# A two-layer decoder trunk: qcT ahead of the turned queries, and the copy of turned probabilities ahead of the row maximum

## The chip, the core and the metric

The kernel runs on one core of a Trainium2 chip. The metric is the device time of one execution in microseconds. A core has five engines with a queue each: PE (TensorE, matmuls and transposes), DVE (VectorE), ACT (ScalarE), POOL (GpSimd) and SP (SyncE, which here issues the weight loads). Each queue runs in order; the program orders work between engines with semaphores written out by hand.

## The reference

Two layers of a decoder, 256 tokens of width 1024, float32. In outline, for layer 0:

```
xn   = rms_norm(h)
q, k, v, qc = split(xn @ w_in)            # 12 query heads, 3 key/value heads, 4 cross heads, 64 wide
q, k = rope(q), rope(k)
self_out  = sliding-window attention (128 keys back) with a sink logit per head
cross_out = softmax(qc . km / 8) vm       # 256 memory tokens, km, vm = rms_norm(mem) @ w_mem_kv
h += rms_norm(concat(self_out, cross_out) @ w_out)
h += rms_norm(silu(xn2 @ w_gate) * (xn2 @ w_up) @ w_down)      # 3584 wide
```

Layer 1 has stick-breaking attention in place of the first one and eight experts of the same width, of which each token uses two, in place of the dense feed-forward part.

## The kernel before

The program is one block of instructions for each engine, written by hand in the order in which the engine runs them. PSUM has eight banks; `Banks` counts how often each was filled and drained. `begin(label, bank)` makes PE wait until the bank's last content was drained, `end` marks it full, and `copy(label, ...)` on ACT or DVE waits until a label is full, moves it to SBUF and marks it empty.

**Layer-0 front end on PE.** PE transposes the normed tokens to xT, multiplies them with column blocks of w_in (labels `qa`, `qb`, `vc`; helper `rows`, line 417), and then makes the queries and keys that attention wants in transposed form. The queries with rope are written by DVE into `rope_q`, which has two buffers, and PE transposes them (line 536) into the banks 5 and 0 by turns: labels `("qT", "a", 0)`, `("qT", "a", 1)`, `("qT", "b", 0)`, `("qT", "b", 1)`; with the b ones come the keys (`("kT", tt)`, line 543). The cross queries need no rope: `turned_cols` (line 428) makes `("qcT", 0)` straight from the weights and xT, in 32 matmuls, in bank 4, between the a and the b transposes. Attention begins when all of these have been copied out (line 548).

**DVE in the front end.** A loop over n = 0 to 3 (line 1394) applies rope to qa and qb, both token tiles. For n of 2 and 3 it must not overwrite rope_q before PE has transposed what is in it:

```
if n >= 2:
    dve.wait_ge(*bk.full(("qT", "a", n - 2)))
ins = dve.tensor_tensor(rope_q[:, n % 2, 0:nq * HD], ...)      # line 1414
```

Then it writes the keys (line 1418) and, after the loop, copies both `kT` to SBUF (line 1256, `copy`).

**Attention of layer 0.** Eight units u (three key/value groups and the cross heads, each for two token tiles); a unit has nk = 1 or 2 blocks of 128 keys: 1, 2, 1, 2, 1, 2, 2, 2. All engines run the units as a pipeline, in steps s:

- PE: scores(s+1) (lines 442 and 450), weigh(s-2) (line 475, values by probabilities), turn_probs(s-1) (line 461, transposes of the probabilities to banks 4 and 5, after `norm_ok` of that unit).
- DVE: row_max(s) (lines 1309 to 1316, then `max_ok`), turned_probs(s-2) (line 1256, bank 5), normalise(s-1) (lines 1322 to 1328, then `norm_ok`).
- ACT: turned_probs(s-2) (line 966, bank 4), the exponentials of s (lines 986 to 990, after `max_ok`), mixed(s-2) (line 966).

normalise(s-1) waits until ACT has taken the exponentials of that unit; the exponentials come after its row maximum. weigh(s-2) waits for both copies of the turned probabilities.

After attention come the output projection (line 417), two norms, and the feed-forward part, in which every float32 weight is cut in two parts by ACT (`w_hi`, line 1025) and DVE (`w_lo`, line 1359) and multiplied in three matmuls (lines 556 to 558). Weights arrive by SP's queue in six slots (`raw`), each of which is loaded again once its content has been used.

Of the kernel before, what the change touches and what calls it, by code (L numbers as in the profile page):

```python
# [5 lines left out]
P = 128  # L6
# [101 lines left out]
def trunk(nc, t):  # L108

    with ExitStack() as ctx:  # L110
# [102 lines left out]
        qcT = mixT[:, 6:8, :]  # L213
# [29 lines left out]
        def probsT(u):  # L243

            return (probsT0 if u < len(UNITS0) else probsT1)[:, u % 2]

        def bank(b, lo=0, hi=512):
            return psum[:, b, lo:hi]
# [97 lines left out]
        def _(pe):  # L346
# [18 lines left out]
            def begin(label, b):  # L365

                s, n = bk.fill(label, b)
                if n > 0:
                    pe.wait_ge(s, n)

            def end(ins, label):
                ins.then_inc(bk.full_sem(label), 1)
# [39 lines left out]
            def rows(label, b, srcT, tt, w, lo, hi, at=0, first=True, last=True):  # L412

                if first:
                    begin(label, b)
                for k in range(KD):
                    ins = pe.matmul(bank(b, at, at + hi - lo), srcT[:, k, tt * P:(tt + 1) * P],  # L417
                                    w.at(k, lo, hi), start=(k == 0), stop=(k == KD - 1))
                if last:
                    end(ins, label)  # L420
                return ins

            def turned_cols(label, b, w, los):

                begin(label, b)
                for i, lo in enumerate(los):
                    for k in range(KD):
                        ins = pe.matmul(bank(b, i * S, (i + 1) * S), w.at(k, lo, lo + P), xT[:, k, :],  # L428
                                        start=(k == 0), stop=(k == KD - 1))
                end(ins, label)  # L430
                return ins
# [80 lines left out]
            w = Block()  # L512
# [3 lines left out]
            w = Block()  # L516
# [3 lines left out]
            w = Block(P)  # L520
            for tt in range(NT):
                rows(("vc", tt), 6 + tt, xT, tt, w, 0, P)
            w.done(("vc", 1))
            pe.wait_ge(consts, 1)

            for n, (tag, tt) in enumerate([("a", 0), ("a", 1), ("b", 0), ("b", 1)]):
                if n == 2:
                    w = Block(2 * P)
                    turned_cols(("qcT", 0), 4, w, (0, P))
                    w.done(("qcT", 0))  # L530
                pe.wait_ge(roped, n + 1)
                label = ("qT", tag, tt)
                begin(label, 5 if n % 2 == 0 else 0)
                b = bk.at[label][0]
                for c in range(4 if tag == "a" else 2):
                    ins = pe.transpose(bank(b, c * P, (c + 1) * P), rope_q[:, n % 2, c * P:(c + 1) * P],
                                       ident[:, :])
                end(ins, label)
                if tag == "b":
                    label = ("kT", tt)  # L540
                    begin(label, 1 + tt)
                    for g in range(NKV):
                        ins = pe.transpose(bank(1 + tt, g * P, (g + 1) * P),
                                           kdup[:, tt, g, :, :].rearrange("p u c -> p (u c)"), ident[:, :])
                    end(ins, label)
# [98 lines left out]
            w = Block()  # L644
# [80 lines left out]
            w = Block()  # L725
# [16 lines left out]
            w = Block()  # L742
# [212 lines left out]
        def _(act):  # L955
# [8 lines left out]
            def copy(label, out, src, scale=None):  # L964
                act.wait_ge(*bk.full(label))
                act.activation(out, src, ACT.Copy, scale=1.0 if scale is None else scale)\  # L966
                    .then_inc(bk.empty_sem(label), 1)
# [80 lines left out]
                           bias=halfpi[:, 0:1]).then_inc(sines, 1)  # L1048
            for tt in range(NT):
                copy(("vc", tt), v[:, tt, 64:192], bank(6 + tt, 0, 128))  # L1050
            for tag in "ab":
                if tag == "b":
                    copy(("qcT", 0), qcT, bank(4).rearrange("p (c s) -> p c s", c=2))
                for tt in range(NT):
                    label = ("qT", tag, tt)
                    n = 4 if tag == "a" else 2
                    copy(label, qT[:, 0:4, tt * P:(tt + 1) * P] if tag == "a" else
                         qT[:, 4:6, tt * P:(tt + 1) * P],
                         bank(bk.at[label][0], 0, n * P).rearrange("p (c s) -> p c s", c=n))
# [33 lines left out]
            for i, (kind, b, half) in enumerate(pieces):  # L1093
                tt = half
# [58 lines left out]
            for u, _, i, tt, *_ in UNITS1:  # L1153
                mixed(u, i, tt)
# [90 lines left out]
        def _(dve):  # L1245
            links = [0]

            def link(ins):

                links[0] += 1  # L1250
                ins.then_inc(dve_chain, 1)
                dve.wait_ge(dve_chain, links[0])

            def copy(label, out, src, scale=None):
                dve.wait_ge(*bk.full(label))
                ins = dve.tensor_copy(out, src) if scale is None else \
                    dve.tensor_scalar(out, src, scale, None, ALU.mult)
                ins.then_inc(bk.empty_sem(label), 1)
# [44 lines left out]
            def row_max(u, layer, i, tt, nk):  # L1303

                K = nk * P
                for b in range(2):
                    dve.wait_ge(*bk.full(("s", u, b)))
                src = psum[:, 2 * (u % 2):2 * (u % 2) + 2, 0:2 * K].rearrange("p b (h k) -> p b h k", h=2)
                link(dve.tensor_reduce(nmax[:, u, :].rearrange("p (h b) -> p b h", b=2), src, AX.X, ALU.max))  # L1309
                if layer == 0 and i < NKV:  # L1310
                    link(dve.scalar_tensor_tensor(out=nmax[:, u, :], in0=nmax[:, u, :], scalar=-SCALE,
                                                  in1=nsinks[:, 4 * i:4 * i + 4], op0=ALU.mult, op1=ALU.min))
                    dve.tensor_tensor(esink[:, u, :], nmax[:, u, :], sinks[:, 4 * i:4 * i + 4], ALU.add)\
                        .then_inc(max_ok, 1)
                else:
                    dve.tensor_scalar(nmax[:, u, :], nmax[:, u, :], -SCALE, None, ALU.mult).then_inc(max_ok, 1)

            def normalise(u, layer, i, nk):
                for b in range(2):
                    dve.wait_ge(*bk.empty(("s", u, b)))  # L1320
                if layer == 0 and i < NKV:
                    link(dve.tensor_tensor(psum_e[:, u, :], psum_e[:, u, :], esink[:, u, :], ALU.add))
                link(dve.reciprocal(recip[:, u, :], psum_e[:, u, :]))
                for b in range(2):
                    for s2 in range(2):
                        x = probs[:, u % 2, b, s2, 0:nk * P]
                        h = 2 * s2 + b
                        ins = dve.tensor_scalar(x, x, recip[:, u, h:h + 1], None, ALU.mult)  # L1328
                ins.then_inc(norm_ok, 1)

            def turned_probs(u, nk):
                copy(("pT", u, 1), probsT(u)[:, 1, :, 0:nk, :],
                     bank(5).rearrange("p (h k q) -> p h k q", h=2, k=2)[:, :, 0:nk, :])

            def attend(units):
                for s in range(len(units) + 2):
                    if s < len(units):
                        u, layer, i, tt, keys = (units[s][x] for x in (0, 1, 2, 3, 6))
                        row_max(u, layer, i, tt, (keys[1] - keys[0]) // P)
                    if s >= 2:  # L1340
                        u, keys = units[s - 2][0], units[s - 2][6]
                        nk = (keys[1] - keys[0]) // P
                        turned_probs(u, nk)
                    if 1 <= s <= len(units):
                        u, layer, i, keys = (units[s - 1][x] for x in (0, 1, 2, 6))
                        normalise(u, layer, i, (keys[1] - keys[0]) // P)
# [30 lines left out]
            a, n = rope_s[:, 0, :, :], rope_s[:, 1, :, :]  # L1377
# [16 lines left out]
            for n, (tag, tt) in enumerate([("a", 0), ("a", 1), ("b", 0), ("b", 1)]):  # L1394
# [3 lines left out]
                x = bank(bb, 0, nh * HD).rearrange("p (h c) -> p h c", c=HD)  # L1398
# [22 lines left out]
            for tt in range(NT):  # L1421
                copy(("kT", tt), kT[:, 0:NKV, tt * P:(tt + 1) * P],
                     bank(1 + tt, 0, NKV * P).rearrange("p (c s) -> p c s", c=NKV))
            attend(UNITS0)

            def lower_f0(tt):
# [20 lines left out]
            for i, (kind, b, half) in enumerate(pieces):  # L1447
                tt = half
# [337 lines left out]
        def _(sp):  # L1786
            for tt in range(NT):
                sp.dma_start(memb[:, tt, :], t["mem"][0, tt * P:(tt + 1) * P, :]).then_inc(mem_in[tt], 16)
            def load(n, src):
                _, c, w = src.shape  # L1790
                sp.dma_start(raw_at(n, c, w), src).then_inc(raw_full[n % RAW], 16)
# [93 lines left out]
```

## Time and profile before

| | |
|---|---|
| three runs | 1522.79, 1524.44, 1525.82 us; median 1524.44 |
| the profiled execution | 1522.79 us, span 1521.1 us |
| busy | PE 1464.3, DVE 1098.4, ACT 934.0, POOL 98.7 us |
| granted PE clock, mean | 0.988 |
| layer-0 attention on DVE | 74.85 us (first maximum) to 102.8 us |
| output projection on PE | 104.61 to 132.3 us |
| PE in attention, a unit of 256 keys | mask 0.60 and scores 1.14, weigh 1.11 us |
| PE's waits ahead of weigh for DVE's copy | 0.22, 0.93, 0.88, 0.88 us (at 84.34, 96.69, 99.83, 102.97) |
| last issue of layer-0 w_in by SP | up to 46.93 us; the 512 KB loads of it landed in 4.3 us (median) |

A row of the timeline has the start (us from the start of the span), the length in us, the engine and line, the operation, what it writes and reads with its shape, how many instructions were merged, and in brackets how long the engine was idle before and what ended that. A row of the windows has the stretch, its length, the busy time of PE, PE's weight loads, DVE, ACT and POOL with the count of instructions, PE's granted clock (1.00 is full), the share of DMA time and GB/s. The chain has start, length and what ran. Waits have the engine and what it waited for: us in total, times, the longest.

### The profile page before, as it was taken

The numbers are of one execution on the slowest core, as the hardware profiler recorded it, in microseconds if no ns is written. First come the engines' busy times: TensorE is split into PE (matmuls) and PEld (weight loads), VectorE is DVE, ScalarE is ACT, GpSimd is POOL, SyncE is SP. The second block draws the span as 40 slices with busy tenths as digits, with TensorE's granted clock in tenths as the row PEclk, the third lists the DMA queues.
The fourth block names the chain that finished last, engine by engine and source line by source line (L and its number), as shares of the span: only waits on it lengthen the run. The fifth ranks groups of instructions, "written<-read, shape, count | busy, mean of one in ns | idle before, by whom it ended". The sixth has DMA issues, their size and how long they took to land.

```text
span 1521.1 us, 18595 instructions
## 1 busy us (share of the span) xinstructions
PE 1464.3 (96%) x6705; PEld 1174.1 (77%) x6705; DVE 1098.4 (72%) x822; ACT 934.0 (61%) x790; POOL 98.7 (6%) x168
## 2 busy tenths in 40 slices
PE   6988999999999789999999999999999999999997
PEld 5555888888877478888888888888888888888885
DVE  3264554544322468989899998988899889989897
ACT  2154434343235347787777777777778778777774
POOL 3001000000000112010010002002001001000000
PEclk9999999999999979999999999999999999999999
DMA  9506555554433259999999999999999999999994
GB/s 342 176 24 221 180 198 189 182 205 139 139 111 111 97 197 389 389 357 400 375 354 400 378 366 384 387 369 377 391 366 374 389 374 368 398 377 354 387 375 162
DMA packets 177595, 446.88 MB, mean 294 GB/s; under 512 B 8784, under 2 KB 17040, under 8 KB 161424
## 3 DMA queue, kind: packets, MB, share of 16 engines
q1 hardware_dynamic: 173584, 432.60, 78.0%
q0 software_dynamic: 3968, 13.69, 2.4%
q8 instruction: 28, 0.46, 0.1%
q14 instruction: 15, 0.12, 0.0%
HBM read 438.37 MB, written 7.90 MB: 293 GB/s over the span
## 4 chain that ended last, share of the span: by engine, by line
PE 90%; DVE 4%; ACT 3%; issue 2%; DMA 1%; POOL 0%; POOLq 0%; SPq 0%; ACTq 0%; DVEq 0%
PE psum L556 24%; PE psum L558 24%; PE psum L557 24%; PE psum L417 5%; PE psum L428 4%; PE psum L875 2%; ACT w_hi L1025 2%; PE psum L782 1%; DVE w_lo L1359 1%; DMA raw<-in_l_w_mem_kv 1%; DVE reg_a L1328 0%; PE psum L383 0%; PE psum L400 0%; DVE nmax L1309 0%; PE psum L807 0%
## 5 line engine op out<-in xcount | busy, mean ns | idle before, releaser
L1359 DVE TENSOR_TENSOR w_lo<-raw,w_hi 128x2048 fp32r<-128x2048 f32 x378 | 861.5, 2290 | 192.2 <-ACT w_hi L1025 191.0
L1025 ACT ACTIVATE w_hi<-raw 128x2048 fp32r<-128x2048 f32 x378 | 724.5, 1919 | 272.8 <-PE psum L558 272.7
L556 PE MATMUL psum<-w_hi,x_hi 128*128 128x512 f32 x1120 | 444.1, 396 | 10.1 <-DVE x_lo L1354 7.6
L558 PE MATMUL psum<-w_hi,x_lo 128*128 128x512 f32 x1120 | 437.9, 391 | 0.0
L557 PE MATMUL psum<-w_lo,x_hi 128*128 128x512 f32 x1120 | 437.2, 390 | 0.0
L556 PEld LDWEIGHTS psum<-w_hi,x_hi 128*128 128x128 f32 x1120 | 211.0, 188 | 55.3 <-DVE x_lo L1354 6.3
L558 PEld LDWEIGHTS psum<-w_hi,x_lo 128*128 128x128 f32 x1120 | 210.8, 188 | 45.0
L557 PEld LDWEIGHTS psum<-w_lo,x_hi 128*128 128x128 f32 x1120 | 211.3, 189 | 42.1
L556 PE MATMUL psum<-w_hi,h_hi 128*128 128x512 f32 x560 | 218.8, 391 | 0.0
L558 PE MATMUL psum<-w_hi,h_lo 128*128 128x512 f32 x560 | 217.9, 389 | 0.0
L557 PE MATMUL psum<-w_lo,h_hi 128*128 128x512 f32 x560 | 217.9, 389 | 0.0
L558 PEld LDWEIGHTS psum<-w_hi,h_lo 128*128 128x128 f32 x560 | 105.1, 188 | 21.9
L557 PEld LDWEIGHTS psum<-w_lo,h_hi 128*128 128x128 f32 x560 | 105.2, 188 | 21.5
L556 PEld LDWEIGHTS psum<-w_hi,h_hi 128*128 128x128 f32 x560 | 105.2, 188 | 21.5
L1767 POOL TENSOR_TENSOR idle<-mhalf 128x1 f32<-128x1 f32 x7 | 15.2, 2170 | 728.2 <-DVE work L1651 728.2
L1633 DVE TENSOR_TENSOR work<-work,psum 128x512 f32<-128x512 f32 x56 | 60.7, 1084 | 0.0
L1354 DVE TENSOR_TENSOR h_lo<-psum,h_hi 128x512 fp32r<-128x512 f32 x70 | 47.8, 684 | 15.0 <-ACT h_hi L1018 15.0
L1215 ACT ACTIVATE work<-psum 128x512 f32<-128x512 f32 x56 | 33.5, 599 | 39.4 <-PE psum L558 39.3
L428 PE MATMUL psum<-reg_b,raw 128*128 128x256 f32 x256 | 56.4, 380 | 0.0
L428 PEld LDWEIGHTS psum<-reg_b,raw 128*128 128x128 f32 x256 | 48.2, 190 | 6.8 <-issue 0.3
L417 PE MATMUL psum<-raw,reg_b 128*128 128x512 f32 (+2 forms) x160 | 52.3, 487 | 1.0 <-ACT reg_b L966 1.0
L1018 ACT ACTIVATE h_hi<-psum 128x512 fp32r<-128x512 f32 x70 | 41.6, 595 | 15.9 <-PE psum L875 10.8
(245 smaller groups left out, 825.9 us busy)
## 6 DMA issues: line engine op xcount, KB each, us to landing
raw<-in_l_w_gate SPq DMA_DIRECT2D x126, 1024.0 KB, 7.5
raw<-in_l_w_up SPq DMA_DIRECT2D x126, 1024.0 KB, 7.6
raw<-in_l_w_down SPq DMA_DIRECT2D x126, 1024.0 KB, 7.2
raw<-in_l_w_in SPq DMA_DIRECT2D x14, 1024.0 KB, 6.5
raw<-in_l_w_out SPq DMA_DIRECT2D x8, 1024.0 KB, 5.1
raw<-in_l_w_mem_kv SPq DMA_DIRECT2D x4, 1024.0 KB, 6.2
ys<-w_lo SPq DMA_DIRECT2D x4, 512.0 KB, 7.1
memb<-in_mem SPq DMA_DIRECT2D x2, 512.0 KB, 3.9
```

The costliest lines, as they stand in the source:

```text
L417: ins = pe.matmul(bank(b, at, at + hi - lo), srcT[:, k, tt * P:(tt + 1) * P], w.at(k, lo, hi), start=(k == 0), stop=(k == KD - 1))
L428: ins = pe.matmul(bank(b, i * S, (i + 1) * S), w.at(k, lo, lo + P), xT[:, k, :], start=(k == 0), stop=(k == KD - 1))
L556: pe.matmul(out, x[0], w[0], start=first, stop=False, skip_group_check=True)
L557: pe.matmul(out, x[0], w[1], start=False, stop=False, skip_group_check=True)
L558: return pe.matmul(out, x[1], w[0], start=False, stop=last, skip_group_check=True)
L875: ins = pe.transpose(bank(7, c * P, (c + 1) * P), hid1[:, b % 2, c * P:(c + 1) * P], ident[:, :])
L1018: act.activation(out, src, ACT.Copy).then_inc(part_hi, 1)
L1025: act.activation(w_hi[:, m % CUT, :], raw[:, n % RAW, :], ACT.Copy).then_inc(hi_ok, 1)
L1215: act.activation(act1[:, b % 2, :], bank(bk.at["g", b][0]), ACT.Silu)\
L1354: dve.tensor_tensor(out, src, high.bitcast(F32), ALU.subtract).then_inc(bk.empty_sem(label), 1)
L1359: dve.tensor_tensor(w_lo[:, m % CUT, :], raw[:, n % RAW, :], w_hi[:, m % CUT, :].bitcast(F32), ALU.subtract).then_inc(lo_ok, 1)
L1633: dve.tensor_tensor(hid1[:, b % 2, :].rearrange("p (c q) -> p q c", c=CB), act1[:, b % 2, :].rearrange("p (q c) -> p q c", c=CB), bank(bk. ...
```

## The change

Two orders are changed; no instruction is added or taken away. On PE the matmuls of `("qcT", 0)` and the wait for their weights come right after `vc`, ahead of the transposes of all rope queries, and ACT copies qcT ahead of all qT. On DVE, in a step of layer-0 attention, the copy of the turned probabilities of unit s-2 comes ahead of the row maximum of unit s.

```
@@ PE
             w.done(("vc", 1))
+            w = Block(2 * P)
+            turned_cols(("qcT", 0), 4, w, (0, P))
+            w.done(("qcT", 0))
             pe.wait_ge(consts, 1)

             for n, (tag, tt) in enumerate([("a", 0), ("a", 1), ("b", 0), ("b", 1)]):
-                if n == 2:
-                    w = Block(2 * P)
-                    turned_cols(("qcT", 0), 4, w, (0, P))
-                    w.done(("qcT", 0))
                 pe.wait_ge(roped, n + 1)
@@ ACT
+            copy(("qcT", 0), qcT, bank(4).rearrange("p (c s) -> p c s", c=2))
             for tag in "ab":
-                if tag == "b":
-                    copy(("qcT", 0), qcT, bank(4).rearrange("p (c s) -> p c s", c=2))
                 for tt in range(NT):
@@ DVE
             def attend(units):
                 for s in range(len(units) + 2):
-                    if s < len(units):
-                        u, layer, i, tt, keys = (units[s][x] for x in (0, 1, 2, 3, 6))
-                        row_max(u, layer, i, tt, (keys[1] - keys[0]) // P)
                     if s >= 2:
                         u, keys = units[s - 2][0], units[s - 2][6]
                         nk = (keys[1] - keys[0]) // P
                         turned_probs(u, nk)
+                    if s < len(units):
+                        u, layer, i, tt, keys = (units[s][x] for x in (0, 1, 2, 3, 6))
+                        row_max(u, layer, i, tt, (keys[1] - keys[0]) // P)
                     if 1 <= s <= len(units):
```

## Rows read from the trace of the kernel before

**Rows 1.** The page: busy time by engine, and the chain by engine.
```profile
PE 1464.3 (96%) x6705; PEld 1174.1 (77%) x6705; DVE 1098.4 (72%) x822; ACT 934.0 (61%) x790; POOL 98.7 (6%) x168
...
PE 90%; DVE 4%; ACT 3%; issue 2%; DMA 1%; POOL 0%; POOLq 0%; SPq 0%; ACTq 0%; DVEq 0%
```

**Rows 2.** Windows of four stretches.
```profile
72.00:74.00 2.00, 0.47 (x5) 0.14 (x4) 1.02 (x2) 1.53 (x2) 0.00 (x0) 1.00 0.90 244
...
138.00:140.00 2.00, 2.00 (x6) 1.62 (x5) 1.73 (x2) 1.08 (x1) 0.38 (x2) 0.50 1.05 397
...
260.00:400.00 140.00, 140.00 (x654) 117.23 (x654) 64.60 (x43) 52.10 (x48) 4.63 (x10) 1.00 0.50 167
700.00:800.00 100.00, 100.00 (x457) 82.68 (x456) 89.18 (x49) 76.69 (x52) 5.77 (x5) 1.00 1.02 372
```

**Rows 3.** Waits over the whole span: SP's longest, and one of PE.
```profile
SPq L1791 <- DVE w_lo L1359: 960.7, 360, 17.9
...
PE psum L475 <- DVE reg_b L1256: 2.9, 4, 0.9
```

**Rows 4.** The chain around qcT and after the output projection.
```profile
63.28 0.87 PE psum L536 x8
64.15 6.91 PE psum L428 x32
...
138.17 0.43 PE psum L557
...
143.19 0.23 PE psum L557
```

**Rows 5.** PE in order of time: transposes, scores, weigh.
```profile
63.12 1.04 PE L536 MATMUL psum<-ident,reg_a 128*128 128x128 f32 x8
...
71.44 0.38 PE L536 MATMUL psum<-ident,reg_a 128*128 128x128 f32 x2
71.66 0.49 PE L543 MATMUL psum<-ident,mixT 128*128 128x128 f32 x3
73.69 0.38 PE L442 MATMUL psum<-band_b,ident_b 128*128 128x256 bf16 x2 [1.53 <-DVE work L1256]
...
79.33 0.66 PE L461 MATMUL psum<-ident,reg_a 128*128 128x128 f32 x4 [0.78 <-DVE reg_a L1328]
...
96.69 1.12 PE L475 MATMUL psum<-reg_b,work 128*64 128x128 f32 x16 [0.93 <-DVE reg_b L1256]
97.86 1.09 PE L461 MATMUL psum<-ident,reg_a 128*128 128x128 f32 x8
...
132.15 1.04 PE L383 MATMUL psum<-ident,xn 128*128 128x128 f32 x8
...
528.72 1.94 PE L383 MATMUL psum<-ident,xn 128*128 128x128 f32 x8 [6.33 <-DVE xn L1272]
```

**Rows 6.** DVE in order of time: ropes, copies, row maximum, scalings.
```profile
63.82 0.43 DVE L1414 TENSOR_TENSOR reg_a<-reg_a 128x256 f32<-128x256 f32 x1 [9.52 <-PE psum L536]
...
66.55 0.62 DVE L1418 TENSOR_TENSOR mixT<-reg_a 128x192 f32<-128x192 f32 x2
72.14 1.02 DVE L1256 COPY work<-psum 128x384 f32<-128x384 f32 x2 [4.97 <-PE psum L543]
...
78.40 0.87 DVE L1328 TENSOR_SCALAR reg_a<-reg_a,recip 128x128 f32<-128x128 f32 x4
79.19 0.68 DVE L1309 TENSOR_REDUCE nmax<-psum 128x4 f32<-128x512 f32 x1
...
96.66 1.14 DVE L1328 TENSOR_SCALAR reg_a<-reg_a,recip 128x256 f32<-128x256 f32 x4
98.99 0.69 DVE L1256 COPY reg_b<-psum 128x512 f32<-128x512 f32 x1 [1.19 <-PE psum L461]
```

**Rows 7.** ACT in order of time: the table load.
```profile
72.27 1.28 ACT L986 ACT_TABLE_LOAD   x1
```

**Rows 8.** Groups by line and shape, 74 to 105 us: busy us, mean ns.
```profile
L990 ACT ACTIVATE reg_a<-psum,nmax 128x256 f32<-128x256 f32 x20 | 9.2, 469 | 0.6 <-DVE nmax L1316 0.5
```

## The prediction

> **What bounds the kernel now.** I read the busy line first: PE is busy for 96% of the span, DVE for 72%, and the chain that ended last is 90% PE, most of it the three matmul lines of the two feed-forward stages [rows 1]. The windows of two such stretches show PE busy for 140.00 of 140 us and for 100.00 of 100 [rows 2]. What SP, which issues the weight loads, waits for longest is DVE's w_lo (960.7 us in 360 waits), that is, for raw slots to come free [rows 3]: the transfers run ahead of the engines there. Those stages have no slack of their own that a later start could use up. They begin when the first layer's attention and output projection are done, so any microsecond added to or taken from the layer-0 front end moves the end of the kernel by one microsecond.
>
> The change touches only that front end, from 63 to 104 us. There I read the chain, then the instructions of PE and of DVE in order of time. From 63.28 to 71.06 us the chain is PE's alone [rows 4]; at 73.69 PE has waited 1.53 us for DVE's copies of kT before the first scores [rows 5]. From 78.40 to 97.8 us it is the other way round: DVE's rows follow each other with no idle time marked [rows 6], while PE and ACT wait for it. Attention is DVE-bound from its third step, s = 2, until step 7: from the scalings of unit 0 (78.40) to those of unit 6 (96.66) six steps take 18.26 us, 3.04 each. Only in steps 8 and 9, where no row maximum is left to do, does DVE idle: 1.19 us ahead of each of the two copies of turned probabilities, the first at 98.99 [rows 6].
>
> **Part A: qcT ahead of the turned queries.** No instruction is added. PE's 32 matmuls of qcT (6.91 us in the chain [rows 4]), which lay between the a and the b transposes, now follow the last vc matmul. The wait that matters is in DVE's rope loop: for n = 2 it waits until ("qT", "a", 0) is full before it writes rope_q again. Before, this was met 0.70 us after the transposes began (63.12 to 63.82), and all the rest of the b ropes, 63.82 to 66.55 + 0.62 = 67.17, 3.35 us, lay under qcT, which lasted until 71.06 [rows 4 to 6]. After, the transposes themselves start only when qcT has ended, and nothing is left to cover the 3.35 us.
>
> Before: in the chain vc ends and the transposes take over at 63.28; scores start at 73.69; 10.41 us. After, step by step from 63.28: qcT 6.91, to 70.19. From there the a transposes until DVE starts, as from 63.28 to 63.82: 0.54, to 70.73. DVE's ropes 3.35, to 74.08. PE wakes (0.06, as between the DVE scaling that ends at 97.80 and the PE row at 97.86 [rows 5, 6]) and does the five transposes of b1 and kT1: 71.44 to 71.66 + 0.49, 0.71 us, to 74.85. DVE copies kT1: the two copies took 1.02, so one 0.51, and it starts within 0.03 us if DVE is awake and within 0.5 us if it starts as slowly as at 72.14; the kT0 copy is done just ahead of it, so I take 0.1, to 75.46. From the end of the copies (73.16) to the scores (73.69) were 0.53 us, the PE queue's row of waits. Scores start at 75.99: **+2.3 us**, between +2.2 and +2.7. What is queued behind the waiting DVE instruction is both ropes of b, both copies of kT and all of attention; behind PE's wait for the ropes, the transposes and all scores. ACT's copy of qcT costs nothing: it moves ahead of the copies of qT a, which are needed only to free bank 5, and this takes two copies of 0.6 us from about 70.3, to 71.5, while b0's ropes end at 70.73 + 1.0 = 71.73. ACT's table load of 1.28 us [rows 7] now comes at about 75, still ahead of the first maximum. The block of w_in that qcT reads was issued by 46.93 us and such a load landed in 4.3 us, so its earlier use at 63.28 is covered too; its raw slots come free 0.9 us earlier, which no one needs.
>
> **Part B: turned probabilities ahead of the row maximum.** Again nothing is added. Per step DVE did row_max(s), turned(s-2), normalise(s-1); now the copy comes first. The copy needs PE's transposes of unit s-2, which can't start before normalise(s-2), the last thing DVE did in the step before. The row maximum (0.68 us for a unit of 128 keys, more for one of 256, and two small instructions) was what DVE did while PE transposed. With the copy at the head of the queue DVE stands still for that time, and row_max(s), normalise(s-1) and then ACT's exponentials stand behind it. The trace shows this price, because steps 8 and 9 already run so: 1.19 us of marked idle, plus 0.08 because successive DVE rows otherwise overlap by that (79.19 against 78.40 + 0.87), 1.27 us for a unit with eight transposes. For one with four, PE's row is 0.66 instead of 1.09 [rows 5], so 0.84. Six units, u = 0 to 5, get the new wait, three of each size: 3 x 1.27 + 3 x 0.84 = **+6.3 us**. If four transposes save half of 1.11 instead, it is 3 x 1.27 + 3 x 0.72 = 6.0. Units 6 and 7 pay what they paid.
>
> Can the displaced work be late next? Row_max(s) ends 1.2 to 1.9 us later in the step, so ACT's exponentials of s do too, but normalise(s) is a whole step further on and they take only some 2 us (four of 0.469 [rows 8], and their small ones). PE must have done scores(s+1) and weigh(s-2) before it can transpose s-1: 1.7 and 1.1 us, against a DVE step of now 3.04 + 1.05 = 4.1 us. Neither comes to bound it. What the new order gives back: PE's weigh waited 2.9 us for DVE's copies in four places [rows 3], two of them of 0.88 us in steps 8 and 9, which stay; the other two (0.93 of it at 96.69 [rows 5]) are 1.15 us together. As DVE and not PE sets the pace there, this is worth nothing, or at most 1.15 us.
>
> **Sum.** 2.3 + 6.2 = +8.5 us. The profiled execution took 1522.79 us (span 1521.1), so 1531.3 for it; it was the fastest of the three, and on the median of 1524.44 the same sum gives **1532.9 us**. Bounds of the terms: 2.2 + 6.0 - 1.15 = +7.1 and 2.7 + 6.3 = +9.0.
>
> **The clock.** PE's granted clock is full (1.00) from 60 to 134 us, also from 72 to 74 us where PE is busy for only 0.47 of 2 us [rows 2]. It falls to 0.5 (1.2 of 2.4 GHz) only after PE stood still for 4.21 us ahead of 137.40, and there 12 matmuls in the chain took 0.43 us each instead of 0.23 [rows 4], 2.4 us. The change thins PE's work: between 71.2 and 76.0 us it will be busy for 1.4 us, and in attention it will idle about 1 us more per step. I take no fall in the sum. The Trainium skill (TensorE: Matmul & The Clock Gate, section "What's actually happening") says that the throttled state is the default and that the gate goes by how busy PE has been recently. By that rule the thinned stretch could fall to 1.2 GHz; by the rows it kept 2.4 GHz through a thin stretch. This gives the first rival.
>
> **Rivals.**
> 1. The clock falls to half in the thinned stretch. Price: 2.4 us if it hits full-length work as at 137 us; if it holds through attention, transposes go from 1.04 to 1.94 us for eight (at 132.15 and, at a granted 0.50, at 528.72 [rows 5]), and they are now on the path six times: 3 x 0.9 + 3 x 0.45 = 4.1. 1535.3 to 1537.0. Against it: the 0.47-busy stretch. 15%.
> 2. The rope wait is covered after all (part A is worth 0), because the b ropes don't truly hang on the late transpose. 1530.7. Against it: DVE's 9.5 us of idle at 63.82, released by just that transpose. 6%.
> 3. Half of part B is hidden, since PE transposes bank 5 late anyway and DVE's idle is shared with another wait. 1524.4 + 2.3 + 3.1 = 1529.8. 8%.
> 4. Not slower: attention's pace is set by PE's weigh, waiting for the copies, and not by DVE. Then the earlier copy removes the 1.15 us of waits above and its own waits cost nothing: 2.3 - 1.15 = +1.2, 1525.6. It decides if a step still takes 3.04 us. Against it: DVE's rows have no gap there and PE waits in them. 6%. Faster than that needs part A to remove PE's 1.53 us wait for kT as well: 3%.
>
> **How the numbers follow.** The forecast has 62%, with a range of its own from 1530 to 1535 (the sum's bounds and the 3 us between the runs shown). About 0.2%, 3 us, is what a measurement of this kernel can tell from no change. Slower: 62 + 15 + 6 + 8 = 91, less one for a forecast gone small, 90%. Within 0.2%: rival 4 and that one, 7%. Faster: 3%. The range reaches down to rivals 2 and 3 and up to rival 1: 1528.5 to 1537.5; outside are rival 4, the faster case and the tails.
>
> **What would show it.** Right: PE's qcT matmuls directly follow vc, at about 63; DVE idles 16 us instead of 9.5 before the first b sum, which starts at about 70.7; the first scores at about 76; DVE's copies of turned probabilities carry idle time released by PE's transposes eight times instead of twice, six of them new, 0.75 or 1.19 us each; the output projection starts at about 113 instead of 104.61; every stage after that is shifted and otherwise equal. Wrong: if the scores start before 75, part A is; if a step of attention still takes 3.04 us and not 4.1, part B is; if the projection is late by 8.5 us and the end is not, the later stages had slack, or the clock's recovery after 140 us differs.

## The result, and the profile after

The changed kernel takes 1535.83 us in the median of five runs (1532.86 to 1542.44), the kernel before 1524.44. The ratio over all its runs is 1.0087 with a 95% interval of 1.0064 to 1.0109, that is +13.3 us on 1524.4, where +8.5 was forecast. Measured again later beside other kernels it was 1536.56 us, ratio 1.0077 (1.0064 to 1.0091). So the direction was right, and the size was too small. The median of the five lies inside the range given; by the ratio the time is 1537.7, and the 34 runs listed for this kernel have a mean of 1537.7 too, just above the range.

The runs point to the clock. Each lists its mean granted PE clock, and over the 34 runs the changed kernel falls into groups, with two exceptions (1538.28 us at 0.985, and the profiled one): 1533 to 1536 us at a clock of 0.985 or 0.986, 1537 to 1538 at 0.981, 1539 to 1540 at 0.979 and 1541 to 1543 at 0.980. The kernel before is at 0.987 to 0.988 in nearly all of its own. The forecast of 1532.9 describes only the fastest executions.

The profiled execution is a slower one, 1540.10 us at a mean clock of 0.981, with a span of 1538.4 us, 17.3 us above the span of before. PE in order of time:

```profile
65.92 7.07 PE L428 MATMUL psum<-reg_b,raw 128*128 128x256 f32 x32
72.83 1.04 PE L535 MATMUL psum<-ident,reg_a 128*128 128x128 f32 x8
74.56 0.44 PE L535 MATMUL psum<-ident,reg_a 128*128 128x128 f32 x2 [0.69 <-DVE mixT L1416]
74.83 0.49 PE L542 MATMUL psum<-ident,mixT 128*128 128x128 f32 x3
76.94 0.44 PE L535 MATMUL psum<-ident,reg_a 128*128 128x128 f32 x2 [1.61 <-DVE mixT L1416]
77.21 0.49 PE L542 MATMUL psum<-ident,mixT 128*128 128x128 f32 x3
78.82 0.59 PE L442 MATMUL psum<-band_b,ident_b 128*128 128x256 bf16 x2 [1.12 <-issue]
...
111.48 1.97 PE L461 MATMUL psum<-ident,reg_a 128*128 128x128 f32 x8 [0.51 <-DVE reg_a L1326]
114.32 2.00 PE L475 MATMUL psum<-reg_b,work 128*64 128x128 f32 x16 [0.88 <-DVE reg_b L1254]
```

These answer to [rows 5]. qcT comes first, then the a transposes. PE waits 0.69, 1.61 and 1.12 us where it waited 1.53 once. The chain shows where vc ends (66.09) and when the projection begins (121.61):

```profile
66.09 6.91 PE psum L428 x32
...
78.82 0.59 PE psum L442 x2
...
111.48 1.98 PE psum L461 x8
...
121.61 3.75 PE psum L417 x7
```

From the end of vc to the first scores it is 78.82 - 66.09 = 12.73 us, where the prediction's steps give 12.71. From the first scores to the projection it is 42.79 us, where it was 73.69 to 104.61, 30.92: +11.87 us, against 6.2 forecast. DVE's rows, answering to [rows 6]:

```profile
73.54 0.42 DVE L1412 TENSOR_TENSOR reg_a<-reg_a 128x256 f32<-128x256 f32 x1 [16.43 <-PE psum L535]
...
85.62 0.87 DVE L1326 TENSOR_SCALAR reg_a<-reg_a,recip 128x128 f32<-128x128 f32 x4
87.25 0.42 DVE L1254 COPY reg_b<-psum 128x256 f32<-128x256 f32 x1 [0.75 <-PE psum L461]
...
91.32 0.69 DVE L1254 COPY reg_b<-psum 128x512 f32<-128x512 f32 x1 [1.19 <-PE psum L461]
...
110.28 1.14 DVE L1326 TENSOR_SCALAR reg_a<-reg_a,recip 128x256 f32<-128x256 f32 x4
113.48 0.69 DVE L1254 COPY reg_b<-psum 128x512 f32<-128x512 f32 x1 [2.06 <-PE psum L461]
```

DVE idles 16.43 us instead of 9.52 before the first b sum, and the new waits of attention are there, 0.75 us three times and 1.19 us three times, as worked out. What was not forecast are the idle times ahead of the last two copies, in steps 8 and 9: 2.06 us in the last row, and 2.82 at 118.25, where both had 1.19. They stand behind transposes that took 1.97 us instead of 1.09. The windows say why (the seventh number after the length is the granted clock):

```profile
66.00:74.00 8.00, 7.87 (x41) 6.75 (x40) 0.46 (x2) 1.24 (x3) 0.00 (x0) 1.00 1.05 392
74.00:78.00 4.00, 1.53 (x10) 1.05 (x10) 3.63 (x11) 1.56 (x5) 0.00 (x0) 1.00 1.05 388
78.00:84.00 6.00, 5.18 (x22) 2.51 (x22) 1.63 (x5) 2.69 (x10) 0.00 (x0) 0.52 0.44 161
84.00:108.00 24.00, 16.72 (x147) 11.66 (x146) 17.52 (x58) 14.78 (x64) 0.00 (x0) 0.98 0.00 1
108.00:122.00 14.00, 10.35 (x66) 8.44 (x66) 5.83 (x15) 4.46 (x14) 0.00 (x0) 0.53 0.00 0
122.00:124.00 2.00, 2.00 (x5) 0.77 (x5) 0.00 (x0) 0.00 (x0) 0.00 (x0) 0.84 0.04 8
124.00:150.00 26.00, 26.00 (x65) 11.60 (x64) 8.29 (x5) 5.95 (x7) 1.48 (x4) 1.00 0.23 80
```

The clock falls twice to half: at the first scores, right after the stretch from 74 to 78 us in which PE was busy for 1.53 of 4 us, and again from 108 us through the last steps of attention into the projection. From 66 us to the second fall PE never waited longer than 1.61 us. After 124 us the later stages are those of before, shifted: the last 138 us of either span have the same granted clock (0.98) and PE busy for 127.47 us here and 127.12 before, and windows of 100 to 300 us from 150 us on, shifted by 17.3 us, agree within 0.1 us of PE's busy time. The 17.3 us are then 2.8 ahead of the change, 2.3 for part A, 11.9 for attention, and 0.3 behind it (the projection begins at the low clock and takes 0.5 us longer). The 2.8 don't belong to the change. They are the start of this one execution: the first weights came 0.6 us later (13.52 us against 12.92), and the first 32 matmuls took 9.36 us where the execution of before had 7.14. Such a start isn't tied to the order: those matmuls took 7.14 us in the profile of part B alone and 9.15 in that of part A alone. In the chain:

```profile
2.10 13.52 DMA raw<-in_l_w_mem_kv
...
15.76 9.36 PE psum L400 x32
```

### The profile page after: what moved, and what is told of

Same layout as the page of the kernel before. It is cut to its first block, busy times and chain, and to the rows that moved or that the text cites. A ratio compares the mean times of both kernels' runs of the same rounds, so it can differ in the third digit from the quotient of the medians.

```text
span 1538.4 us, 18595 instructions
## 1 busy us (share of the span) xinstructions
PE 1474.6 (96%) x6705; PEld 1180.7 (77%) x6705; DVE 1098.7 (71%) x822; ACT 933.9 (61%) x790; POOL 98.2 (6%) x168
## 4 chain that ended last, share of the span: by engine, by line
PE 90%; DVE 4%; ACT 3%; issue 2%; DMA 1%; POOL 0%; POOLq 0%; SPq 0%; ACTq 0%; DVEq 0%
PE psum L555 24%; PE psum L557 23%; PE psum L556 23%; PE psum L417 5%; PE psum L428 4%; PE psum L874 2%; ACT w_hi L1024 2%; PE psum L781 1%; DVE w_lo L1357 1%; DMA raw<-in_l_w_mem_kv 1%; PE psum L461 1%; PE psum L400 1%; DVE nmax L1307 0%; DVE reg_a L1326 0%; PE psum L383 0%
## 5 line engine op out<-in xcount | busy, mean ns | idle before, releaser
L555 PE MATMUL psum<-w_hi,x_hi 128*128 128x512 f32 x1120 | 444.0, 396 | 10.1 <-DVE x_lo L1352 7.6
```

The lines of the kernel that those rows point to most:

```text
L555: pe.matmul(out, x[0], w[0], start=first, stop=False, skip_group_check=True)
```

## The experiments

Times are medians; ratios are to the kernel before, which ran beside each group of experiments on the same chip (15 to 18 runs, medians 1524.29 to 1524.57 us) and five times beside the first run of the changed kernel.

| run | us | ratio (95%) | us over before | PE clock in its runs |
|---|---|---|---|---|
| changed kernel | 1535.83 | 1.0087 (1.0064 to 1.0109) | +13.3 | 0.979 to 0.986 |
| changed kernel again | 1536.56 | 1.0077 (1.0064 to 1.0091) | +11.7 | 0.980 to 0.986 |
| A alone | 1528.60 | 1.0030 (1.0019 to 1.0040) | +4.6 | 0.984 to 0.986 |
| B alone | 1534.95 | 1.0066 (1.0053 to 1.0080) | +10.1 | 0.982 to 0.986 |
| A, own buffers | 1524.82 | 1.0007 (0.9998 to 1.0016) | +1.1 | 0.987, 0.988 |
| A, filled | 1527.56 | 1.0020 (1.0011 to 1.0028) | +3.0 | 0.987, 0.988 |
| B, filled | 1531.46 | 1.0041 (1.0029 to 1.0054) | +6.3 | 0.988 |
| both, filled | 1533.70 | 1.0063 (1.0049 to 1.0076) | +9.6 | 0.988, 0.989 |
| both, rope waits filled | 1540.57 | 1.0103 (1.0088 to 1.0119) | +15.7 | 0.980, 0.981 |
| both, attention filled | 1536.65 | 1.0087 (1.0074 to 1.0101) | +13.3 | 0.985 to 0.987 |
| qcT last | 1523.02 | 0.9993 (0.9984 to 1.0002) | -1.1 | 0.987 to 0.989 |
| qcT last, filled | 1518.76 | 0.9957 (0.9943 to 0.9971) | -6.6 | 0.992 to 0.996 |
| the same, filled more | 1516.91 | 0.9947 (0.9934 to 0.9960) | -8.1 | 0.994 to 0.998 |

**Each part alone.** Part A alone is the first two blocks of the diff, part B alone the third.

> Part A alone (qcT ahead of the turned queries; attention in the old order). Theory 1, the terms add: the first scores start 12.7 us after the last vc matmul instead of 10.4, attention itself takes its 30.9 us (first scores to output projection) unless PE's clock falls in the thin stretch before the first scores; 1526.7 on a median of 1524.4, up to 1529 if the clock falls there for some 5 us. Theory 2, part A alone costs the clock: over 1530. Rival, the rope wait is covered: 1524.

> Part B alone (copy of turned probabilities ahead of the row maximum). Theory 1: first scores unchanged, attention 6.2 us longer, 37.1 us, 1530.6, six new idle times of 0.75 and 1.19 us on DVE. Theory 2, it is the thinner attention that lets the clock fall at its end: granted clock 0.50 in part of the last 15 us before the projection and in its first matmuls, up to 4 us more, 1534 to 1535. Rival, B is hidden: 1524.

Both showed more than their waits. Of part A's profile, the chain and a window:

```profile
65.00 6.91 PE psum L428 x32
...
77.74 0.58 PE psum L442 x2
...
110.74 14.40 PE psum L417 x33
```

```profile
80.00:84.00 4.00, 4.00 (x20) 2.23 (x18) 2.00 (x5) 1.60 (x9) 0.00 (x0) 0.53 0.01 5
84.00:88.00 4.00, 2.56 (x21) 1.55 (x21) 3.76 (x18) 3.74 (x19) 0.00 (x0) 1.00 0.00 0
```

With part A alone the first scores are 12.74 us behind vc, 2.3 more than before. Attention, whose order is that of before, takes 33.00 us instead of 30.92; 2.1 us go to the clock of 0.53 in its first steps. It recovers by 84 us, and the end keeps 1.00. In part B's profile, the windows of the later steps, the projection's beginning, and PE's rows there:

```profile
72.00:88.00 16.00, 10.44 (x91) 6.78 (x91) 10.69 (x34) 9.16 (x40) 0.00 (x0) 1.00 0.38 133
88.00:102.00 14.00, 9.44 (x84) 6.59 (x84) 10.44 (x31) 8.85 (x38) 0.00 (x0) 0.98 0.01 1
102.00:118.00 16.00, 13.22 (x68) 9.31 (x66) 4.53 (x14) 4.17 (x13) 0.00 (x0) 0.50 0.00 1
```

```profile
73.49 0.38 PE L442 MATMUL psum<-band_b,ident_b 128*128 128x256 bf16 x2 [1.53 <-DVE work L1256]
...
99.58 1.09 PE L461 MATMUL psum<-ident,reg_a 128*128 128x128 f32 x8 [1.22 <-DVE reg_a L1328]
...
104.05 1.97 PE L461 MATMUL psum<-ident,reg_a 128*128 128x128 f32 x8 [0.51 <-DVE reg_a L1328]
...
114.19 16.05 PE L417 MATMUL psum<-raw,mixT 128*128 128x512 f32 x32 [0.52 <-issue]
```

Attention takes 114.19 - 73.49 = 40.70 us, 9.8 more than before: 6.4 up to the scalings of unit 6 (102.86) for the waits, and 3.4 behind them for the clock, which is at half from about 102 us on. It stays there into the projection, which takes 2.1 us longer too. So each part brings a fall of its own: A the one at the first scores, B the one at the end.

**The waits without the clock.** The direct test fills PE's waits with transposes of the identity into a bank that nobody is using. Nobody reads them.

```
def warm(n, b):
    for _ in range(n):
        pe.transpose(bank(b, 0, P), ident[:, :], ident[:, :])
...
warm((0, 0, 5, 13)[n], 6)          # ahead of wait_ge(roped, n + 1); 8 more ahead of the waits before attention
...
if s in (0, 1): warm(5, 5)         # ahead of scores
warm(6, 4)                         # ahead of wait_ge(norm_ok) in turn_probs, 3 for two of the units
warm(7, bb)                        # ahead of weigh's waits for the two cross-head units
```

> The changed kernel, with 92 transposes of the identity that nobody reads put on PE where it would wait: 26 around the rope waits, the rest in attention. If the clock is what the sum lacked: granted clock 1.00 from 60 us to the end of the projection, and the sum without a clock term holds, +8.5 us, 1533, with runs closer together than the 9.6 us between the five of the changed kernel; perhaps 0.5 to 1 us more where a filler is still running when its wait ends. Rival, something else than the clock: the runs stay between 1533 and 1542, or all are slower by the filler's 10 us, 1548.

> Part A alone with fillers around the rope waits and in the first two steps of attention. If part A is 2.3 us of waits and the rest of its 4.5 us is the clock: granted clock 1.00 from 60 to 134 us and 1524.4 + 2.3 = 1526.7. Rival: 1528.6 as without fillers.

> Part B alone with the 66 fillers in attention. If part B is 6.2 us of waits and the rest of its 10.1 us is the clock: granted clock 1.00 through attention and the projection, 1524.4 + 6.2 = 1530.6, six new idle times on DVE of the same 0.75 and 1.19 us. Rival: 1534.5 as without fillers.

The same four stretches with both parts and all fillers:

```profile
72.00:88.00 16.00, 14.98 (x128) 11.02 (x128) 10.58 (x33) 8.41 (x33) 0.00 (x0) 1.00 0.36 133
88.00:102.00 14.00, 11.96 (x110) 8.52 (x106) 10.79 (x37) 8.46 (x37) 0.00 (x0) 1.00 0.00 1
102.00:118.00 16.00, 13.38 (x107) 9.68 (x106) 6.32 (x17) 5.90 (x21) 0.00 (x0) 1.00 0.01 2
118.00:130.00 12.00, 12.00 (x30) 5.30 (x29) 0.71 (x1) 1.11 (x2) 0.66 (x2) 1.00 0.00 0
```

The granted clock stays at 1.00, and the changed kernel becomes faster by doing 92 transposes more: 1533.70 us, with all five runs between 1531.60 and 1535.78. The intervals of the two ratios overlap; the means, 1533.5 us of these five and 1537.6 of all 40 runs of the changed kernel, are clearly apart. Part A comes to +3.0 us and part B to +6.3, of which the waits were to be 2.3 and 6.2.

The profiles tell waits, clock and fillers apart. Attention is cut here at the first of the scalings (line 1328 of before) of unit 0 and of unit 6; "projection" runs from its first matmul to the transposes behind it (132.15 in [rows 5]). All in us:

| profile | end of vc to scores | to unit 0 | to unit 6 | to projection | projection |
|---|---|---|---|---|---|
| before | 10.41 | 4.71 | 18.26 | 7.95 | 27.54 |
| A alone | 12.74 | 6.81 | 18.26 | 7.93 | 27.54 |
| B alone | 10.41 | 4.71 | 24.66 | 11.33 | 29.63 |
| both | 12.73 | 6.80 | 24.66 | 11.33 | 28.05 |
| both, filled | 12.74 | 5.30 | 24.67 | 8.14 | 27.55 |
| both, rope waits filled | 12.77 | 4.71 | 26.48 | 11.33 | 29.69 |
| both, attention filled | 12.74 | 7.94 | 24.67 | 8.14 | 27.55 |

The waits are the first column (+2.3) and the third (+6.4), and they stay when the clock is held up. The clock is in the second (+2.1, part A's), the fourth (+3.4, part B's) and the last. Of these, the filled kernel keeps 0.6 and 0.2 us, which is what the fillers cost. In the filled part B the six waits on DVE are 0.75 and 1.19 us, as without fillers:

```profile
83.04 0.42 DVE L1268 COPY reg_b<-psum 128x256 f32<-128x256 f32 x1 [0.75 <-PE psum L469]
87.11 0.69 DVE L1268 COPY reg_b<-psum 128x512 f32<-128x512 f32 x1 [1.19 <-PE psum L469]
```

**One of the two stretches filled.** The view tested here is that the two falls are separate, each with its own filler.

> The changed kernel with only the 26 filler transposes around the rope waits. If two separate falls of the clock make up what the sum lacked, this one takes away the first (at the first scores, part A's, 1.7 us) and leaves the second (at the end of attention, part B's, 4 us): granted clock 1.00 until about 100 us, 0.50 in the last steps; 1524.5 + 8.5 + 4 = 1537, up to 1538. If the first fall alone is the cause: 1533.

> The changed kernel with only the 66 filler transposes in attention (from the second unit's scores on). It leaves the fall at the first scores, and takes away the one at the end: 1524.5 + 8.5 + 1.7 = 1534.7, between 1533.5 and 1536. If the end's fall is triggered by the first one and not by the thin steps themselves, it would differ from this by nothing, but the run with only the rope filler would then come out at 1533.

Both missed. With only the rope waits filled the kernel gained nothing, 1540.57 us; its interval (1.0088 to 1.0119) overlaps that of the changed kernel, so it isn't shown to be slower either. Its profile shows the first fall not gone but moved into attention, and one more ahead of the one at the end:

```profile
76.00:80.00 4.00, 3.52 (x30) 2.53 (x31) 1.96 (x4) 1.67 (x2) 0.00 (x0) 1.00 0.98 357
80.00:84.00 4.00, 2.19 (x20) 1.27 (x17) 3.01 (x11) 3.05 (x16) 0.00 (x0) 1.00 0.03 9
84.00:88.00 4.00, 4.00 (x22) 2.13 (x20) 2.74 (x10) 2.45 (x14) 0.00 (x0) 0.57 0.00 0
88.00:92.00 4.00, 3.15 (x38) 2.45 (x34) 2.65 (x8) 1.13 (x4) 0.00 (x0) 1.00 0.02 4
92.00:96.00 4.00, 2.94 (x14) 1.77 (x14) 3.11 (x14) 3.52 (x18) 0.00 (x0) 0.78 0.00 2
96.00:100.00 4.00, 4.00 (x34) 2.87 (x33) 1.68 (x4) 1.49 (x6) 0.00 (x0) 0.79 0.00 0
```

Thin steps follow on the filled stretch, PE is busy for 2.19 of 4 us, and in the next 4 us the clock is at 0.57. In the table the second column is that of before, and the third is 1.8 us longer than with both unfilled. With only attention filled the fall at 76 to 82 us stays and the end keeps 1.00, as expected, but the time is 1536.65 us, 2 above what was expected. The table places it: waits 8.7 us instead of 8.5, the fall 2.1 instead of 1.7, and 1.3 for the fillers, most of it because the first of them run at half the clock too (7.94 us where the changed kernel has 6.80). That makes 12.2 us, 1536.5.

**Part A without its wait.** The b queries get their own buffer, and DVE's wait of line 1412 goes:

```
+        rope_qb = mixT[:, 3:5, :]
...
-                if n >= 2:
-                    dve.wait_ge(*bk.full(("qT", "a", n - 2)))
```

> Part A alone, but the b queries with rope get a buffer of their own in an unused piece of mixT, so DVE's loop doesn't wait for the a transposes. If the rope wait is all of part A's cost: b ropes are done before qcT ends, first scores 10.4 us after vc, as before; 1524.4, no thin stretch and no clock term. Rival, the order itself costs (ACT's copies, the weight block): 1526.7 as in part A alone.

1524.82 us, and the interval holds 1. In the profile the clock stays at 1.00 and attention takes 30.91 us as before; from the end of vc to the scores it is 10.58 us, where before had 10.41, as one transpose now waits 0.39 us for ACT. So the rope buffer is nearly all of part A's cost, its share of the clock too, and the order itself costs 0.2 us in the profile; by the runs it could be up to 2.4 us.

**A better order, and fillers where they pay.** In the old attention, qcT goes last: own buffer for the b queries, all transposes of queries and keys first, qcT under DVE's copies of kT, and PE waits for qcT's copy only ahead of unit 6.

> The kernel before with qcT after all transposes of ropes instead of between them: the b ropes have a buffer of their own, PE makes all queries and keys first, then qcT, under which DVE copies kT; PE waits for qcT's copy only ahead of the scores of the cross heads. Attention in the old order. If the sum's view of the front end is right, PE's wait of 1.53 us for kT goes and the scores start about 1.4 us earlier: 1523.1, with PE denser and no fall of the clock; within the noise of a measurement. Rival: ACT's copies and table load now end the wait: 1524.5.

> The same with fillers, transposes of the identity that nobody reads, at PE's long waits outside attention: 34 at the start, 34 after the first output projection, 110 around the router of layer 1. Theory, the clock is worth time wherever PE works on the chain just after a wait: the 12 slow matmuls at 137 us (2.4 us), the half-speed transposes, router and gather matmuls from 528 to 549 us (up to 6 us), and the slow start in some executions; 7 to 9 us faster than without, 1514 to 1517. Rival: the fillers end late and give back what they gain, or the clock there doesn't follow them: 1523.

> qcT last with the fillers outside attention, more of them at the start and at the router, and 32 in the thin steps of layer-0 attention (first two, last ones). 1 to 3 us faster than with fillers outside attention alone (1518.8) if they keep the clock at 80 to 84 us, where it fell to 0.57: 1516 to 1518. Rival: no better, 1519, as each filler also delays what comes behind it.

qcT last gains 1.1 us, not told apart from nothing. In its profile too the clock falls for a while, 0.82 and 0.76 in the mean of the windows from 76 to 80 and from 80 to 84 us. The scores start 9.24 us after vc instead of 10.41, and the fall gives the 1.2 us back: attention, in the order of before, takes 32.14 us instead of 30.92. Nearly all that has changed lies ahead of it; that the dense qcT directly ahead of the thin first steps is the reason is a guess. With the fillers outside attention it is 1518.76 us, ratio 0.9957: the expected direction, but 4.3 us (5.5 by the ratios) where 7 to 9 were expected. After the first output projection PE's rows show a filler at work:

```profile
134.62 3.88 PE L390 MATMUL psum<-ident 128*128 128x128 f32 x34
139.00 0.47 PE L565 MATMUL psum<-w_hi,x_hi 128*128 128x512 f32 x1 [0.51 <-DVE x_lo L1368]
139.31 0.40 PE L566 MATMUL psum<-w_lo,x_hi 128*128 128x512 f32 x1
139.54 0.40 PE L567 MATMUL psum<-w_hi,x_lo 128*128 128x512 f32 x1
```

The matmuls start 0.23 us apart from the second on, where they ran at 0.43 in [rows 4] until 142.66. With more fillers, in the thin steps of attention as well, the clock is 1.00 at 80 to 84 us, where it was 0.57 without those, and it is 1516.91 us, ratio 0.9947 (0.9934 to 0.9960): 0.5% faster than the kernel before and the fastest of all here. How much of it comes from which filler was not tried.

**The changed kernel again.**

> The changed kernel again, unchanged, beside the others on one chip: 1533 to 1542 with the faster runs at the higher granted clock; a mean of 1537.5, and where the profile of the earlier run showed two falls of the clock, this one shows the second at least.

Ratio 1.0077; six runs from 1535.14 to 1542.51, in the same groups of clock (0.985 or 0.986, 0.981 or 0.982, 0.980), and its profile has both falls, at 78 to 84 and from about 108 us on, in a span of 1540.8 us. Attention takes 42.81 us there, as in the first profile (42.79), but the clock stays at half until 124 us, and the projection takes 29.59 us, 2.1 more than before. Another 1.7 us come behind it, as they do in the profile of part B alone; their cause is open.

## Why the prediction was too low

- **The place and the direction were right.** The change is paid between 63 and 122 us, and all stages behind are shifted and keep their length. Nothing later absorbs it.
- **Part A's waits were right**: 12.71 us from vc to the scores worked out, 12.73 and 12.74 measured, and DVE's sum starts 0.54 us behind qcT, as was taken. Shown also by the run with own buffers, which takes the wait away and with it the cost. Rival 2 is out.
- **Part B's waits were right**: 0.75 and 1.19 us at six places, +6.3 us worked out (taken as 6.2 in the sum), +6.4 in the profiles with the clock at 1.00 and without. Rivals 3 and 4 are out.
- **The step that failed is the sentence "I take no fall in the sum".** The clock's term was mis-sized: 0 was taken. In the two profiled executions it is 5.5 us in attention, 2.1 at the first scores and 3.4 in the last steps, and 0.5 and 2.1 us more in the projection. Over the runs it is less: by the ratios of the changed kernel without and with fillers 13.3 - 9.6 = 3.7 us (2.1 by the second measurement), and with the 0.8 us that the fillers cost 3 to 4.5. No profile shows an execution of the group of 1533 to 1536 us, so which fall is shorter there stays open. Rival 1 had the mechanism and got 15%. Its price, 2.4 to 4.1 us, was too low for the profiled executions: the 4.1 counted the transposes alone, and the scores, the weighing (2.00 us instead of 1.11) and the projection's first matmuls slowed down too. The case against it rested on one window of 2 us in which the clock held at 0.47 us of work. That row shows only that this one thin stretch brought no fall. After the change the thin stretch is twice as long (1.53 us of work in 74 to 78), and the thinner attention goes on for over 20 us.
- **The range was short for the same reason.** Its upper end was rival 1's. The range also took the 3 us between the runs of before for those of after. The changed kernel has the clock differently from one execution to the next, and its runs spread over 10 us where those of before spread over 3 to 6.5.

## What to carry to other kernels

When a change puts waits on PE, look at the granted clock as a term of the sum and not as a remark: a stretch of PE work that becomes thinner, with waits of only 1 to 2 us, can run at half the clock, and what the waits cost and what the clock costs are told apart by filling the waits with work that nobody reads (which itself cost 0.8 us here). An instruction that waits for the work released by the instruction just ahead of it in the same queue gives up all cover; put something independent between them, as the old order of DVE's step did. A buffer written in a loop with a wait on its reader can hold up a reordering that is otherwise free: giving it a second place took part A from +4.6 us to +1.1, not told apart from nothing.

## What the runs showed of the hardware

- The clock fell to half without a long stop of PE. In the changed kernel the longest wait from 66 us to the second fall was 1.61 us, and PE was busy for 16.72 of 24 us ahead of that fall. In the profile of before two falls, at 136 and at 525 us, came with stops of 4.21 us (the row below) and 6.33 us [rows 5]. The Trainium skill (TensorE: Matmul & The Clock Gate, section "A second HAM failure mode: psum-queue depth-cycling") tells of a kernel in which short idle times between groups of matmuls, if frequent, make the clock swing between its two levels. The traces here agree, with waits for DVE and ACT in place of that kernel's: 0.52 at 78 to 84 us, 0.98 at 84 to 108 and 0.53 at 108 to 122.

```profile
137.40 0.77 PE L556 MATMUL psum<-w_hi,x_hi 128*128 128x512 f32 x1 [4.21 <-DVE x_lo L1354]
```

- More work on PE made the kernel faster: 92 transposes added and 3.7 us less by the ratios, 4.1 by the means of all runs; in the fastest kernel the mean granted clock rose from 0.988 to between 0.994 and 0.998.
- Filling only one thin stretch can move the fall instead of removing it: with the rope waits filled it went from the first scores to the steps behind them, and nothing was gained. And with qcT last the clock fell in an attention whose order is that of before, where it had kept 1.00. So where the clock falls depends on what lies next to a stretch as well. Which stretch of work decides was not settled here.
